# A hybrid decoder layer on one core: tile 0 sent ahead through the trunk, dense gates scattered by indirect DMA, memory placed by address

## The reference

```python
def peer_ffn(h, wq, keys, u_tab, v_tab):
    q = (hf @ wq).reshape(t, PEER_HEADS, 2, PEER_DKEY // 2)
    scores = jnp.einsum("thcd,hcnd->thcn", q, keys)
    s_top, i_top = lax.top_k(scores, PEER_TOPK)                # 16 of 128, twice
    cand = s_top[:, :, 0, :, None] + s_top[:, :, 1, None, :]   # 16 x 16 sums
    best, pos = lax.top_k(cand..., PEER_TOPK)
    gates = jax.nn.softmax(best, axis=-1)
    act = gelu(einsum("thkd,td->thk", u_tab[eidx], x))
    return einsum("thk,thkd->td", gates * act, v_tab[eidx])
```

## Time and profile before

| | |
|---|---|
| time, median of 3 runs | 1761.0 us (1756.67 to 1763.8) |
| the profiled execution | 1757.0 us, span 1755.3 us |
| mean granted TensorE clock | 0.967 |
| PE busy | 1598.4 us (91%) |
| PE weight loads | 1352.1 us (77%) |
| DVE busy | 1218.9 us (69%) |
| ACT busy | 660.7 us (38%) |
| POOL busy | 506.8 us (29%) |
| DMA | 402.98 MB, mean 230 GB/s |

### The profile page before, as it was taken

One profiled execution on the slowest core, in us unless ns is written; L12 is line 12 of the kernel. 1 busy time (PEld: TensorE's weight loads), 2 busy tenths in 40 slices (PEclk: granted clock), 3 DMA queues, 4 the chain that ended last, 5 costly groups with the idle time before them and its releaser, 6 DMA issues.

```text
span 1755.3 us, 26062 instructions
## 1 busy us (share of the span) xinstructions
PE 1598.4 (91%) x7931; PEld 1352.1 (77%) x7931; DVE 1218.9 (69%) x2080; ACT 660.7 (38%) x1039; POOL 506.8 (29%) x612
## 2 busy tenths in 40 slices
PE   8999889899898998888987798866999999999998
PEld 4877445369887898878987688866888888888886
DVE  4403523118999877998779967756887878888885
ACT  2103445114433365433563246622333333333332
POOL 4542002000042311223211221244653433444340
PEclk9899789999999999999998999998999999999999
DMA  5222040011497755998558895599999999999995
GB/s 205 72 72 92 6 156 1 0 60 49 122 297 226 232 192 176 293 303 270 179 187 241 255 322 186 187 371 331 371 396 339 342 335 344 352 361 353 354 349 207
DMA packets 187082, 402.98 MB, mean 230 GB/s; under 512 B 16272, under 2 KB 114576, under 8 KB 186512
## 3 DMA queue, kind: packets, MB, share of 16 engines
q1 hardware_dynamic: 150160, 268.02, 44.9%
q0 software_dynamic: 36864, 134.23, 21.8%
HBM read 347.67 MB, written 54.53 MB: 229 GB/s over the span
## 4 chain that ended last, share of the span: by engine, by line
PE 35%; DVE 25%; issue 7%; ACT 6%; DMA 2%; SPq 1%; ACTq 1%; DVEq 1%; POOL 0%; POOLq 0%
PE psum L972 30%; DVE ulo L1534 5%; PE psum L534 5%; DVE urow L1539 4%; DVE hotB L1645 3%; ACT uhi L1212 2%; ACT hotB L1239 2%; SPq L359 1%; DVE cand L1610 1%; DVE cand L1613 1%; ACT stage L1248 1%; DVE routed L1616 1%; DMA urow<-in_u,idx 1%; DVE h2row L1539 1%; DVE itop L1579 1%
## 5 line engine op out<-in xcount | busy, mean ns | idle before, releaser
L534 PE MATMUL psum<-hhi,uhi 128*128 128x384 f32 x1024 | 358.9, 351 | 37.6 <-ACT uhi L1212 37.6
L534 PE MATMUL psum<-hlo,uhi 128*128 128x384 f32 x1024 | 352.6, 344 | 0.0
L1309 ACT ACTIVATE vhi<-vraw 128x1024 fp32r<-128x1024 f32 x128 | 136.0, 1062 | 305.1 <-PE psum L972 298.7
L534 PE MATMUL psum<-hhi,ulo 128*128 128x384 f32 x1024 | 207.1, 344 | 44.8 <-DVE ulo L1534 44.5
L1534 DVE TENSOR_TENSOR ulo<-h2T,uhi 128x1024 fp32r<-128x1024 f32 x128 | 156.8, 1225 | 122.6 <-ACT uhi L1212 117.0
L972 PE MATMUL psum<-vhi,wlo 128*128 128x512 f32 x768 | 236.5, 389 | 0.0
L972 PE MATMUL psum<-vlo,whi 128*128 128x512 f32 x768 | 236.4, 389 | 0.0
L972 PE MATMUL psum<-vhi,whi 128*128 128x512 f32 x768 | 236.4, 389 | 0.0
L534 PEld LDWEIGHTS psum<-hhi,uhi 128*128 128x128 f32 x1024 | 201.1, 196 | 42.6 <-ACT uhi L1212 42.5
L534 PEld LDWEIGHTS psum<-hhi,ulo 128*128 128x128 f32 x1024 | 179.9, 190 | 57.9 <-DVE ulo L1534 57.7
L516 POOL DMA_INDIRECT urow<-in_u,idx x96 | 106.9, 1113 | 391.9 <-DVE urow L1539 377.1
(11 more groups left out here) (258 smaller groups left out, 2269.6 us busy)
## 6 DMA issues: line engine op xcount, KB each, us to landing
h2T<-in_uT SPq DMA_DIRECT2D x128, 512.0 KB
vraw<-in_v SPq DMA_DIRECT2D x128, 512.0 KB
acts_scratch<-act_s SPq DMA_DIRECT2D x128, 192.0 KB
gring<-gates_scratch SPq DMA_DIRECT2D x128, 192.0 KB
aring<-acts_scratch SPq DMA_DIRECT2D x128, 192.0 KB
gates_scratch<-wring SPq DMA_DIRECT2D x24, 512.0 KB
gates_scratch<-stage SPq DMA_DIRECT2D x24, 512.0 KB
wring<-in_chunks SPq DMA_DIRECT2D x23, 512.0 KB, 4.0
```

The source lines that it names most:

```text
L534: return nc.tensor.matmul(out, lhsT, rhs, start=start, stop=stop)
L1309: a_(vhi[:, k, :], vraw[:, k, :], ACT.Copy).then_inc(s["vhi_ready"], 1)
```

## The change

Five things at once.

1. **Tile 0 goes ahead.** Its stick-breaking attention (`stick0`, all six heads of its 128 tokens together) becomes four steps among `STEPS`. The six heads that follow cover tiles 1 to 3 alone, in 1152 columns. Between them are written tile 0's output projection, residual, normalisation, transposes, queries and key scores, all in PSUM bank 7. Its routing (`route(0)`) runs on DVE from the third head on, and DVE's work for the remaining heads, the residuals and the splits of h2 hangs in its gaps (`beside_route0`).
2. **40 of the 128 dots of tile 0** are taken before the routing of tile 1, between the splits of wq. The row ring has eight buffers instead of four, and the index is read from `eidx` without a copy. Splits and dots are spread evenly over 52 places of each routing: 28 splits and 16 dots with each of tiles 1, 2 and 3, and after them one dot with each of the last 40 splits.
3. **Gates by scatter.** The one-hots, the gate matmuls, ACT's weighing and staging and the 48 stores are gone. `gates_scratch` is set to zero by eight DMAs of 3.1 MB between the chunk loads. After each of the routings 1 to 3, POOL issues 128 indirect DMAs, one per (head, choice), each writing 128 elements of 4 bytes; the 16 of one head wait until those of the head before have landed. As the writes overwrite, DVE first computes in `totals` for each choice of head h the sum of all gates of earlier heads with the same expert, so that the last one written holds the total. Gathers for tile 0 are written between these groups: two per group for tiles 1 and 2, four for tile 3.
4. **Rings of four** for `uhi` and `ulo`, with ACT two blocks ahead; its loop and DVE's are written out.
5. **Memory by address**: every buffer is placed by an offset in KiB (`at`). That lets wout load when the chunk ring falls free, before the heads; wq loads after the state-space part is mixed, behind tile 0's x.

```diff
-R = [(0, 2), (2, 8), (12, 17), (21, 25)]
-H = [(8, 12), (17, 21), (25, 29)]
-H_STEPS = [16 // (b - a) for a, b in H]
+R_SCORES = [0, 4, 11]
+UR = 8
+EARLY_DOTS = 40
+LOWERED = [0, 28, 28, 28]
+DOTTED = [EARLY_DOTS, 16, 16, 16]
+TICKS = 52
+STEPS = [("ssd", 0, 0), ("mem", 0, 0), ("sb", 0, 0), ("mem", 0, 1), ("ssd", 0, 1), ("sb", 1, 0), ("mem", 0, 2), ("mem", 0, 3),
+         ("sb", 2, 0), ("mem", 0, 4), ("ssd", 0, 2), ("mem", 1, 0), ("sb", 3, 0), ("mem", 1, 1), ("ssd", 0, 3), ("mem", 1, 2),
+         ("mem", 1, 3), ("mem", 1, 4)]
...
+                if n in ZERO_AT:
+                    rows = NK * P // (P * len(ZERO_AT))
+                    sp.dma_start(gates_d.rearrange("(p i) j t -> p (i j) t", p=P)[:, rows * ZERO_AT.index(n):rows * (ZERO_AT.index(n) + 1), :],
+                                 zeros.unsqueeze(1).broadcast_to([P, rows, TD])).then_inc(s["gates_zero"], 16)
...
+            def gather(table, n, used, at):
+                k = n % UR
+                if n >= UR:
+                    pool.wait_ge(row_in[k], 16 * (n // UR))
+                    pool.wait_ge(s[used], at)
+                g.indirect_dma_start(urow[k], None, table, bass.IndirectOffsetOnAxis(eidx[:, n % HK:n % HK + 1], 0)).then_inc(row_in[k], 16)
...
+            def put_gates(tt, h):
+                if h:
+                    pool.wait_ge(placed[tt], 16 * TOPK * h)
+                for k in range(TOPK * h, TOPK * (h + 1)):
+                    g.indirect_dma_start(flat, bass.IndirectOffsetOnAxis(sidx[:, tt, k:k + 1], 0), sgate[:, tt, k:k + 1],
+                                         None).then_inc(placed[tt], 16)
+            pool.wait_ge(s["eidx_ready"], 1)
+            pool.wait_ge(s["gates_zero"], 16 * len(ZERO_AT))
+            pool.wait_ge(s["ymix_sb"], SC)
+            gather_u(UR - 1)
+            pool.wait_ge(s["h2row_ready"], NT)
+            gather_u(UR + sum(DOTTED[:2]) - 2)
+            for t in range(1, NT):
+                pool.wait_ge(s["routed_ready"], t + 1)
+                n = gathered[0]
+                for h in range(PH):
+                    put_gates(t - 1, h)
+                    if t < NT - 1:
+                        gather_u(n + DOTTED[t + 1] * (h + 1) // PH)
+                    else:
+                        gather_u(n + 4 * (h + 1))
+            gather_u(HK)
...
+            def totals(t, raw, room):
+                raw_ = raw.rearrange("p h k -> p (h k)")
+                for pair in ((1, 7), (2, 6), (3, 5), (4,)):
...
+                    link(*[v.tensor_tensor(eq, routed[:, 0, n:n + TOPK].unsqueeze(2).broadcast_to([P, TOPK, n]),
+                                           routed[:, 0, 0:n].unsqueeze(1).broadcast_to([P, TOPK, n]), ALU.is_equal)
+                           for h, n, eq in same])
...
+                    link(*[v.tensor_tensor(eq, eq, raw_[:, 0:n].unsqueeze(1).broadcast_to([P, TOPK, n]), ALU.mult)
+                           for h, n, eq in same])
...
+                    link(*[v.tensor_reduce(sm[:, 1, h, :], eq, AX.X, ALU.add) for h, n, eq in same])
...
+            not_kept(0)
+            residual(0)
+            not_kept(1)
+            residual(1)
+            normal(0)
+            argument(0)
+            not_kept(2)
+            argument(1)
             route(0)
+            normal(3)
+            lower_h2(4)
+            lower_h2(5)
+            for h in range(PH):
+                up_to(0, EARLY_DOTS * h // PH)
+                lower_wq(h)
+            up_to(0, EARLY_DOTS)
...
             for t in range(1, NT):
                 route(t)
-                hot(t - 1)
             v.memset(zr[:].bitcast(F32), 0.0).then_inc(s["zero_ready"], 1)
+            while lowered[0] < NK - 4:
+                left = NK - 4 - lowered[0]
+                up_to(lowered[0] + 1, dotted[0] + -(-(HK - dotted[0]) // left))
```

More of the change, by code:

```diff
@@ L810, in _ @@
+            values(2)
+            scores(5)
+            kept(4)
+            values(3)
+            kept(5)
+            values(4)
             pe.wait_ge(s["z_read"], SB_H)
+            project(2, early)
+            project(3, early)
+            values(SB_H - 1)
             pe.wait_ge(s["arg_ready"], SB_H)
-            project(0, early)
-            values(SB_H - 1)
-            for n in range(1, 4):
-                project(n, early)
+            project(4, early)
+            project(5, early)
@@ new lines, in _ @@
+            for i in range(SC):
+                act.wait_ge(s["ysb_ready"], i + 1)
+                a_(sqs[:, i, :], ysb[:, i, :], ACT.Square).then_inc(s["sqy_ready"], 1)
+            act.wait_ge(s["sbss_full"], 1)
+            link(a_(rbB[:], psum[:, 0, 0:TD], ACT.Ln, scale=1.0 / SB_W, bias=eps[:, 0:1]))
+            a_(rbB[:], rbB[:], ACT.Exp, scale=-0.5).then_inc(s["rbB_ready"], 1)
+            normal(1)
+            act.wait_ge(s["soft_in"], 1)
+            a_(sm[:, 1], sm[:, 0], ACT.Exp).then_inc(s["soft_out"], 1)
@@ L1214, in activations @@
-            def activations(k, q):
-                before = (k - 1) % 4
-                act.wait_ge(s["p1_done"], 4 * q + (k + 2))
-                act.wait_ge(act_stored[before], 16 * q + (16 if k else 0))
-                a_(act_s[:, before, :], psum[:, before % 2, 0:TD], ACT.Gelu).then_inc(s["act_ready"], 1)
-            def tile(k, q):
-                upper_u(k, q)
-                if not (isinstance(q, int) and q == 0 and k == 0):
-                    activations(k, q)
-            def tiles(a, b):
-                if a == b:
-                    return
-                with act.Fori(a, b) as q:
-                    for k in range(4):
-                        tile(k, q)
@@ L1299, in _ @@
[L1299 removed]
+            copies = {4 * R_SCORES[t - 1] + 1 + i: (t, i) for t in range(1, NT) for i in range(PH // 2)}
+            softs = {SOFT_AT[t]: t for t in range(1, NT)}
+            for i in range(AHEAD):
+                upper_u(i)
+            for i in range(NK - 4):
+                if i in copies:
+                    key_scores(*copies[i])
+                if i in softs:
+                    softmax(softs[i])
+                tile(i)
             act.wait_ge(s["dot_ready"], HK)
```

1045 lines of the change are left out of this document (522 added, 523 removed).

## The result

The changed kernel takes 1939.3 us (median of 4 runs, 1930.6 to 1960.2), the kernel before 1762.4 (4 runs, 1756.7 to 1764.4): ratio 1.099, 95% interval 1.093 to 1.105. It is slower by 10%; 1672 was forecast, with a range of 1590 to 1745, and 0.14 given to slower. The profiled execution took 1934.1 us, with a span of 1932.3.

A forecast was written before the change was run, and what follows sets the result against it. DVE bounded the part before PE's down stage; POOL would be late next. Routing 1 at 453 + 133 = 586, + 513 (POOL) = 1099, + 27 = 1126, + 541.8 = 1668 span: 1672 us, range 1590 to 1745.

The forecast's parts named there:

- What bounds the kernel, and the down stage: PE's final down matmuls, 541.8 us with the tail, stay untouched; what counts is when the first one starts.
- DVE and PE by themselves: From tile 1's routing, these engines alone need 567 us; DVE sets three stages of about 133 us each.
- POOL's queue: After routing 1, 450 scatter and gather issues on POOL last 513 us, against 434 us for DVE and PE.
- The end of the stage: From POOL's last issue to the first down matmul: row landing, dot, split and last up blocks, 27 us.
- The head: Before routing 1: zero writes free, tile 0's key scores at 290, routing 0 done at 381, routing 1 at 453.
- rival (c): Tile 0's early work stretches the heads or rows arrive late: 20 to 65 us, 1717 at 45; chance 0.13.
- (b): Slower than before: a scatter or its landing costs more than a gather; 1822 us at 1.52 each; chance 0.14.
- Rival (a): POOL keeps pace at 0.98 us an issue, 441 us for 450: time 1597, or 1587 with shorter head; chance 0.24.
- The two rules: Skill statements: tensor_tensor does not stall descriptor generation (0.98 us per issue); DMA writes below 512 B are read-modify-write.
- What would show it: Profile signs: scatters about 1.1 us, POOL gapless from 586 to 1100, routing 1 near 453; wrong if after 480.

The follow-up runs named there:

- run 8: Changed kernel with only POOL's order altered, all rows of u gathered before the last 96 scatters: 1859.9 us.
- the pause run: Changed kernel with a short POOL fill and a wait for it after every scatter: 1906.0 us.
- the 16-index run: Changed kernel with each scatter taking only its first 16 of 128 partitions: 1798.5 us.
- run 2: Changed kernel with each scatter replaced by POOL fills of a spare SBUF tile, no DMA issued in its place: 1834.0 us.
- run 1: Changed kernel without its 384 scatters and the waits on them, gates left zero: 1613.3 us.
- run 4: Changed kernel with each scatter writing 128 rows of 512 bytes to even distances, and one more POOL wait between tiles: 1936.0 us.
- run 7: Changed kernel with each scatter made a plain POOL DMA of 128 4-byte elements to consecutive addresses, without indices: 1722.7 us.
- run 12: The order of run 8, plus a short POOL fill and wait after every scatter: 1901.7 us.
- Run 13: The order of run 8, with the last tile's 128 scatters and the wait on them left out: 1701.2 us.

## Why the prediction was wrong, point by point

**What bounds the kernel, and the down stage.** Right. The down stage takes 541.9 us from its first matmul, as before; all depends on when it starts.

**DVE and PE by themselves.** Right. I had 567 us from the start of routing 1; without scatters it is 1069.6 - 499.1 = 570.5. A stage on DVE was forecast at 133 us and runs from 498 to 630, 132.

**POOL's queue (513 us).** This step failed, and it decided the sign. It was to last 513 us; 450 issues took from 630.6 to 1339.6, 709 us. Taken from start to start, 450 x 1.275 = 574; what 95 of them, at 1.35 to 5 us, have above that (DVE's interference and the waits between groups) is 77; what 8 over 5 us have above it is 59. My 513 were 450 x 0.97 = 436, 65 of interference and 12 of group waits, and these two are 77 as well. That they agree is in part luck: I had one issue per two-input operation of DVE, run 8 shows one per two of them and has 96 us of it, and in the changed kernel DVE often stands still. What failed is that a queue is priced from start to start, and I added up busy times. Between two issues lie 0.305 us, 450 x 0.305 = 137 us in all, and 513 + 137 + 59 = 709. A sign of it was there to see: the first single issue of the earlier trace rows ends with 0.29 us of idle time, which the row puts down to the copy ahead of it. With the 137 us in it, the sum would have been 1263 and the change slower; nothing else was needed for the sign. The landing was not the trouble: where nothing stands between two groups, in run 8, the next issue comes 2.41 us after the last instead of 1.275, so 1.1 us a group against my 0.5; in the changed kernel the gathers between two groups cover it but for 3.3 us in all.

**Starvation (not in the sum at all).** Worth 65 to 80 us, an estimate made in three ways: the pause run freed of its pauses, 1906 - 42 = 1864, is 75 below 1939; the 16-index run has 1.312 us from start to start where after has (574 + 77) / 450 = 1.446, and 1798.5 + 450 x 0.134 = 1859 is 80 below; the run without DMAs needs 384 x 1.37 + 66 x 1.3 = 612 us of queue against 651, and 1834 + 39 = 1873 is 66 below. I see no row of before that shows it: its gathers are held apart by a copy, a wait on a semaphore and the ring's release.

**The end of the stage (27 us).** 51: 1339.6 to 1390.4. In the pause run, without starvation, it is 1331.1 to 1361.5, 30.

**The head.** The zeros beside the input projections cost nothing, as forecast: PE's chain there is one piece of 130 us. Key scores of tile 0 come at 299 (forecast 290), routing 0 ends at 415 (381): DVE is busy 72 of 113 us there, so it waits 41 us where I had 14, mostly in turns with ACT and PE in the heads. The rows land late: the first dot starts at 426.6, and the row issued at 421.6 lands 15.3 us later, at 437, beside the 2 MB store of x1 and the first u blocks. The dots end at 495. Routing 1 starts at 498 instead of 453 and ends at 630 instead of 586. That is rival (c) at its 45 us.

**The sum of the misses**: 44 (head) + 137 (queue) + 59 (its gaps) + 24 (end) = 264, from 1126 to 1390.4.

**The rivals.** (b), slower, came true, and 117 us beyond its figure of 1822. Its mechanism, POOL as the only engine that matters, is most of what happened (221 of the 326 us, by run 2), and its point of no gain, 1.36 us an issue, was passed at 1.45; but the reason is not what the case named. Gathers have the same pitch (0.94 + 0.30 us), and 4 bytes cost as much as 512. What I held for a risk of the unseen writes was a misreading of the rows that I had. Rival (a) rested on 0.98 an issue and falls with it: not even the kernel without scatters (run 1, 1613) gets to 1597.

**The two rules.** The earlier trace rows showed issues stretched under two-input DVE operations, and run 8 confirms it: 1.97 us under dots and splits, 0.97 as soon as DVE stops. So the inference in the Trainium skill, "SBUF — State Buffer", section "Who interferes with whom", that tensor_tensor leaves descriptor generation alone doesn't hold here. The other rule in the Trainium skill, "DMA: Bandwidth & Descriptors", section "Specifications", read-modify-write below 512 B, has no bearing on the indirect DMAs here: writes of 512 bytes (run 4) take as long as writes of 4. The plain writes of 4 bytes in run 7 do fill the DMA engines; whether that rule is the reason no run shows.

**What would show it.** Scatters were to be 1.0 to 1.3 us (1.14: within), POOL without gaps to 1100 (with gaps, to 1340), routing 1 not after 480 (498: the sign of a wrong head). The signs that I had named for the queue were on the busy time again, and so missed what mattered.

**What stays open.** Why long runs of indirect DMAs with 64 or 128 indices starve PE, DVE, ACT and SP, why a short wait behind each prevents it (but for 20 us in run 12), and why run 8's order does. The instruction queues' own transfers are few in both cases (35 packets in one queue after, 28 before). A version that beats both kernels was not found. Run 13 leaves one tile's gates out at 1701 us. Writing that tile's gates by one-hots as before would bring back a third of 146 us on DVE and of 95 us on PE; if PE's 32 us alone lie on the path, that is an estimate of 1733 us, under 2% better than the kernel before, and it was not tried.

## What to carry to other kernels

Price a queue by the time from one start to the next, not by the busy time of an operation: the gap of 0.30 us that looks like nothing beside one DMA was 137 us in 450. When a change moves work from a loaded engine to an idle one, multiply it out there before anything else, with the gap and with the interference in it: 450 x 1.45 us was 651 us beside 440 us of other work. And try another order in such a queue: with the rows that others wait for ahead of the last scatters, 79 of the 177 us came back, though mostly because the starvation went, which I hadn't foreseen.

## What the runs showed of the hardware that I had not expected

- An indirect DMA on POOL costs 0.97 us and 0.30 us until the next can start, whether it reads or writes, 4 or 512 bytes an index (gathers of 4 KB rows: 0.94 and 0.30); 16 indices instead of 128 save 0.13 us. A plain one with 128 elements of 4 bytes costs 0.53 us, but fills the DMA engines (share 1.0).
- Long unbroken runs of them with 64 or 128 indices (47 in a row from 831 us in the changed kernel) leave PE one matmul per 2.8 us (its gaps are mostly 1.62, 2.32 and 3.02 us, in steps of 0.70), stop DVE for up to 47 and ACT for up to 58 us, and the granted clock falls to 0.52, the lower of its two levels for nearly all of that stretch. 16 indices, or a fill of 0.13 us with a wait behind each, which adds 0.11 us, end it; a fill of 0.09 us without the wait doesn't. In run 8, whose runs are of 17 at most, it doesn't appear.
- Under back-to-back two-input operations of DVE an issue takes 1.97 us, one per two operations; beside an idle DVE it takes 0.97.
